# The first unit of weights in quarters on two queues, ones multiplied until the data come, and the first sine layer at another place

## The reference

```
h = rmsnorm(x, norm_mix)
p = h @ w_in                              # 2048 x 4352
h_fwd, h_bwd = implicit_filters(feat, t, w1, b1, fr1, w2, b2, fr2, w3)
#   h = sin(fr1 * (feat @ w1 + b1));  h = sin(fr2 * (h @ w2 + b2));  h = h @ w3;  times a decay
y_a = pool mixer(p[..., :512]);  y_b = hyena mixer(p[..., 512:2816], h_fwd, h_bwd)
y_c = spatial gating(p[..., 2816:])
x = x + concat(y_a, y_b, y_c) @ w_out
x = x + (silu(gate) * val) @ ffn_w_down   # gate, val: width-3 convolutions of rmsnorm(x) @ ffn_w_up
```

## Time and profile before

| | us |
|---|---|
| median of 3 runs | 2247.59 (2247.53 to 2249.07) |
| the profiled execution | 2247.37 |
| its span | 2244.9 |
| TensorE busy in the span | 2206.8 (98%) |

### The profile page before, as it was taken

How to read it: one execution, slowest core, us unless ns; L and a number is a source line. 1 busy time by engine, 2 the same in 40 slices (tenths; PEclk the granted TensorE clock), 3 DMA queues, 4 the chain that set the end, 5 groups by cost and what they waited for, 6 DMA issues and landing times.

```text
span 2244.9 us, 28087 instructions
## 1 busy us (share of the span) xinstructions
PE 2206.8 (98%) x11758; PEld 1883.9 (84%) x11758; DVE 1306.1 (58%) x1593; ACT 1013.3 (45%) x1227; POOL 46.5 (2%) x55
## 2 busy tenths in 40 slices
PE   7999999999999999999999999999999999999998
PEld 6888788888888888888898889878888888888886
DVE  7757547777777775444655555446555555444444
ACT  5443336555555544333654444444433334433333
POOL 1030000000000000000001000000000000000000
PEclk9999999999999999999999999999999999999999
DMA  8444555655555555555464445545666665555552
GB/s 301 158 150 150 182 190 172 204 191 188 189 189 189 190 191 191 192 189 187 142 203 152 151 150 187 183 157 169 188 189 189 189 190 191 193 192 188 188 187 94
DMA packets 267214, 407.55 MB, mean 182 GB/s; under 512 B 6566, under 2 KB 246230, under 8 KB 248657
## 3 DMA queue, kind: packets, MB, share of 16 engines
q1 hardware_dynamic: 264672, 395.47, 53.7%
q0 software_dynamic: 1696, 8.97, 1.1%
q10 hardware_dynamic: 720, 1.32, 0.2%
HBM read 403.64 MB, written 2.10 MB: 181 GB/s over the span
## 4 chain that ended last, share of the span: by engine, by line
PE 94%; DVE 2%; ACT 2%; issue 1%; DMA 1%; DVEq 0%; SPq 0%; ACTq 0%
PE bank L1351 33%; PE bank L1362 17%; PE bank L1386 11%; PE bank L1391 11%; PE bank L1387 11%; PE bank L1354 2%; PE bank L1355 2%; PE bank L1364 2%; DMA raw<-in_w_in 1%; ACT whi L388 1%; DVE wlo L677 1%; PE bank L1241 1%; PE bank L1191 0%; PE bank L1242 0%; ACT M L406 0%
## 5 line engine op out<-in xcount | busy, mean ns | idle before, releaser
L677 DVE TENSOR_TENSOR wlo<-raw,whi 128x2048 fp32r<-128x2048 f32 (+1 forms) x374 | 857.2, 2293 | 815.6 <-ACT whi L388 815.6
L388 ACT ACTIVATE whi<-raw 128x2048 fp32r<-128x2048 f32 (+1 forms) x374 | 715.8, 1916 | 833.2 <-PE bank L1391 446.6
L1351 PE MATMUL bank<-hh,whi 128*128 128x512 f32 x3392 | 825.1, 396 | 14.0 <-ACT whi L388 10.9
L1351 PEld LDWEIGHTS bank<-hh,whi 128*128 128x128 f32 x3392 | 626.5, 189 | 145.9 <-ACT whi L388 10.9
L1362 PEld LDWEIGHTS bank<-hh,wlo 128*128 128x128 f32 x3392 | 429.9, 188 | 17.2
L1362 PE MATMUL bank<-hh,wlo 128*128 128x256 f32 x3392 | 434.8, 281 | 0.0
L1386 PE MATMUL bank<-whi,hh 128*128 128x512 f32 x1088 | 430.6, 396 | 0.0
L1387 PE MATMUL bank<-whi,hh 128*128 128x512 f32 x1088 | 429.0, 394 | 0.0
L1391 PE MATMUL bank<-wlo,hh 128*128 128x512 f32 x1088 | 274.3, 394 | 0.0
L1386 PEld LDWEIGHTS bank<-whi,hh 128*128 128x128 f32 x1088 | 205.5, 189 | 48.6 <-issue 0.2
L1387 PEld LDWEIGHTS bank<-whi,hh 128*128 128x128 f32 x1088 | 205.7, 189 | 46.5
(11 more groups left out here) (221 smaller groups left out, 922.6 us busy)
## 6 DMA issues: line engine op xcount, KB each, us to landing
raw<-in_mlp_w SPq DMA_DIRECT2D x128, 1024.0 KB, 5.4
raw<-in_ffn_w_up SPq DMA_DIRECT2D x88, 1024.0 KB, 5.0
raw<-in_ffn_w_down SPq DMA_DIRECT2D x44, 1024.0 KB, 4.8
raw<-in_w_in SPq DMA_DIRECT2D x34, 1024.0 KB, 5.3
raw<-in_fox_w_in SPq DMA_DIRECT2D x32, 1024.0 KB, 5.3
raw<-in_fox_w_in SPq DMA_DIRECT2D x16, 1032.0 KB, 5.3
raw<-in_w_out SPq DMA_DIRECT2D x16, 1024.0 KB, 4.8
raw<-in_fox_w_out SPq DMA_DIRECT2D x16, 1024.0 KB, 4.8
```

What stands on the lines that cost most here:

```text
L388: e.activation(whi[i % RING][:, 0:n], raw[i % RAW][:, 0:n], ACT.Copy).then_inc(s_hi, 1)
L677: e.tensor_tensor(wlo[i % RING][:, 0:n], raw[i % RAW][:, 0:n], whi[i % RING][:, 0:n].bitcast(F), ALU.subtract).then_inc(s_lo, 1)
L1351: e.matmul(bank[b][:, :], wh[:, k, s], hh[:, kk, :], start=kk == 0, stop=False)
```

## The change

The loads: unit 0 comes as four DMAs of two chunks each on SyncE's queue, X's first half as four DMAs of two chunks each on ScalarE's queue, behind the sixteen columns of the first gain and ahead of the rest of `cols`. ScalarE and VectorE split X and unit 0 quarter by quarter, and TensorE waits for each quarter of unit 0. Unit 1 is split ahead of the second half of X, and the squares come after all of X: four of them, unit 2, the other four. TensorE starts with 32 matmuls of ones. `first_r` goes to place 3 ahead of `filter1`'s matmul. The work of VectorE and ScalarE for the two sine layers is cut from `filter1` and `filter2` and put at places 4 and 6 (`sine1`, `sine2`); TensorE's matmuls stay at 3 and 5. The features and filter weights have a semaphore of their own.

```diff
-    1: [("split", 4), ("spread", 0)], 2: [("total", 0)], 3: [("filter1", 0)], 4: [("first_r", 0)], 5: [("filter2", 0)], 7: [("filter3", 0)],
+    1: [("split", 4), ("spread", 0)], 2: [("total", 0)], 3: [("first_r", 0), ("filter1", 0)], 4: [("sine1", 0)], 5: [("filter2", 0)],
+    6: [("sine2", 0)], 7: [("filter3", 0)],
...
 def sync
-            e.dma_start(X[:, 0:4, :], A["x"][:, 0:4, :]).then_inc(s_x[0], 16)
-            load(0)
-            e.dma_start(X[:, 4:8, :], A["x"][:, 4:8, :]).then_inc(s_x[1], 16)
+            src = units[0][0]
+            for m in range(4):
+                e.dma_start(raw[0][:, 512 * m:512 * m + 512].rearrange("p (k c) -> p k c", k=2), src[:, 2 * m:2 * m + 2, :]).then_inc(
+                    s_w0[m] if m < 3 else s_raw[0], 16)
             load(1)
...
 def scalar
-                    elif what in ("filter1", "filter2"):
-                        o = what == "filter2"
+                    elif what in ("sine1", "sine2"):
+                        o = what == "sine2"
...
-            e.dma_start(cols[:, :], A["cols"]).then_inc(s_col, 16)
+            e.dma_start(cols[:, 0:KD], A["cols"][:, 0:KD]).then_inc(s_gmix, 16)
+            for q in range(4):
+                e.dma_start(X[:, 2 * q:2 * q + 2, :], A["x"][:, 2 * q:2 * q + 2, :]).then_inc(s_x[q], 16)
+            e.dma_start(cols[:, KD:NCOL], A["cols"][:, KD:NCOL]).then_inc(s_col, 16)
             e.wait_ge(s_ones, 1)
             sqrt_table()
+            for q in range(4):
+                s = slice(512 * q, 512 * q + 512)
+                e.wait_ge(s_x[q], 16)
+                high(q, "mix")
+                e.wait_ge(s_w0[q] if q < 3 else s_raw[0], 16)
+                e.activation(whi[0][:, s], raw[0][:, s], ACT.Copy).then_inc(s_hi0 if q < 3 else s_hi, 1)
+            done[0] = 1
+            split(1)
+            for q in range(4, 8):
+                e.wait_ge(s_x[2 + q // 2], 16)
+                high(q, "mix")
             for q in range(8):
                 square(q, piece(q))
+                if q == 3:
+                    split(2)
...
 def vector (low and the subtraction quarter by quarter in the same way), then
+            for q in range(1, 8):
                 add_square(q)
+                if q == 3:
+                    split(2)
...
-                    elif what == "filter1":
-                        e.wait_ge(s_const, 80)
+                    elif what == "sine1":
                         sine(4, col("filt", 0, 64), col("filt", 1, 64))
...
-                    elif what == "filter2":
+                    elif what == "sine2":
                         sine(5, col("filt", 2, 64), col("filt", 3, 64))
...
 def tensor
+            e.wait_ge(s_ones, 1)
+            for _ in range(32):
+                e.matmul(bank[7][:, 0:P], onesr[:, :], onesr[:, :], start=True, stop=True)
```

More of the change, by code:

```diff
@@ L226, in two_block_program @@
         s_hi, s_lo, s_unit = sem("s_hi"), sem("s_lo"), sem("s_unit")
-        s_x = [sem(f"s_x{q}") for q in range(4)]
+        s_x = [sem(f"s_x{q}") for q in range(6)]
+        s_w0 = [sem(f"s_w0{m}") for m in range(3)]
+        s_hi0, s_lo0, s_gmix, s_feat = sem("s_hi0"), sem("s_lo0"), sem("s_gmix"), sem("s_feat")
         s_col, s_id, s_const, s_decay, s_fscale, s_edge, s_ln, s_bs, s_again, s_fox = (
@@ L309, in load @@
                 e.dma_start(dst, src).then_inc(s_raw[i % RAW], 16)
-            e.dma_start(X[:, 0:4, :], A["x"][:, 0:4, :]).then_inc(s_x[0], 16)
-            load(0)
-            e.dma_start(X[:, 4:8, :], A["x"][:, 4:8, :]).then_inc(s_x[1], 16)
+            src = units[0][0]
+            for m in range(4):
+                e.dma_start(raw[0][:, 512 * m:512 * m + 512].rearrange("p (k c) -> p k c", k=2), src[:, 2 * m:2 * m + 2, :]).then_inc(
+                    s_w0[m] if m < 3 else s_raw[0], 16)
             load(1)
-            e.dma_start(X[:, 8:12, :], A["x"][:, 8:12, :]).then_inc(s_x[2], 16)
-            e.dma_start(X[:, 12:16, :], A["x"][:, 12:16, :]).then_inc(s_x[3], 16)
+            e.dma_start(X[:, 8:12, :], A["x"][:, 8:12, :]).then_inc(s_x[4], 16)
+            e.dma_start(X[:, 12:16, :], A["x"][:, 12:16, :]).then_inc(s_x[5], 16)
             for i in range(2, NU):
@@ L331, in gpsimd @@
             e.dma_start(ident[:, :], A["ident"]).then_inc(s_id, 16)
-            for dst, src in ((fe[0:33, :], A["feat"]), (f1, A["filt"]), (w3, A["w3"]), (CS, A["cs"]), (wpool, A["pool_w"])):
+            for dst, src in ((fe[0:33, :], A["feat"]), (f1, A["filt"])):
+                e.dma_start(dst, src).then_inc(s_feat, 16)
+            for dst, src in ((w3, A["w3"]), (CS, A["cs"]), (wpool, A["pool_w"])):
                 e.dma_start(dst, src).then_inc(s_const, 16)
@@ L458, in side @@
                     if what == "spread":
+                        e.wait_ge(s_col, 16)
                         root(1, rb[:, :])
@@ L557, in joined @@
                     square_sum(stage, q, Xt[:, h, 512 * j:512 * j + 512])
-            e.dma_start(cols[:, :], A["cols"]).then_inc(s_col, 16)
+            e.dma_start(cols[:, 0:KD], A["cols"][:, 0:KD]).then_inc(s_gmix, 16)
+            for q in range(4):
+                e.dma_start(X[:, 2 * q:2 * q + 2, :], A["x"][:, 2 * q:2 * q + 2, :]).then_inc(s_x[q], 16)
+            e.dma_start(cols[:, KD:NCOL], A["cols"][:, KD:NCOL]).then_inc(s_col, 16)
             e.wait_ge(s_ones, 1)
             sqrt_table()
-            e.wait_ge(s_col, 16)
-            for q in range(8):
[L564 to L573, removed]
+            e.wait_ge(s_gmix, 16)
+            for q in range(4):
[9 more added lines that the diff above has]
+                high(q, "mix")
+            for q in range(8):
                 square(q, piece(q))
+                if q == 3:
+                    split(2)
             for g, (kind, j, _) in enumerate(IN_GROUPS):
@@ L1040, in joined @@
                 turned(3, gname)
-            e.wait_ge(s_col, 16)
-            for q in range(8):
-                e.wait_ge(s_x[q // 2], 16)
+            e.wait_ge(s_gmix, 16)
+            for q in range(4):
+                s = slice(512 * q, 512 * q + 512)
+                e.wait_ge(s_x[q], 16)
                 low(q, "mix")
[L1046 to L1052, removed]
+                e.wait_ge(*((s_hi0, q + 1) if q < 3 else (s_hi, 1)))
+                e.tensor_tensor(wlo[0][:, s], raw[0][:, s], whi[0][:, s].bitcast(F), ALU.subtract).then_inc(s_lo0 if q < 3 else s_lo, 1)
+            done[0] = 1
+            split(1)
+            for q in range(4, 8):
+                e.wait_ge(s_x[2 + q // 2], 16)
+                low(q, "mix")
+            for q in range(1, 8):
                 add_square(q)
+                if q == 3:
+                    split(2)
             for g, (kind, j, _) in enumerate(IN_GROUPS):
@@ L1259, in side @@
                     elif what == "filter1":
-                        e.wait_ge(s_const, 80)
+                        e.wait_ge(s_feat, 32)
                         e.matmul(bank[4][0:64, 0:T], f1[0:33, 0:64], fe[0:33, :], start=True, stop=True).then_inc(s_fmm, 1)
@@ L1270, in side @@
                         e.wait_ge(s_sin, 2)
+                        e.wait_ge(s_const, 48)
                         e.wait_ge(s_bytok, 1)
@@ L1340, in unit @@
                 wl = wlo[u % RING][:, 0:8 * cw].rearrange("p (k c) -> p k c", k=8)
-                e.wait_ge(s_hi, u + 1)
+                if u:
+                    e.wait_ge(s_hi, u + 1)
                 for k in range(8):
                     kk = half * 8 + k
+                    if u == 0:
+                        e.wait_ge(*((s_hi0, k // 2 + 1) if k < 6 else (s_hi, 1)))
                     if lows is not None:
@@ L1355, in unit @@
                             e.matmul(o, hlo[:, kk, s], wh[:, k, :], start=False, stop=False)
-                e.wait_ge(s_lo, u + 1)
+                if u:
+                    e.wait_ge(s_lo, u + 1)
                 for k in range(8):
                     kk = half * 8 + k
+                    if u == 0:
+                        e.wait_ge(*((s_lo0, k // 2 + 1) if k < 6 else (s_lo, 1)))
                     for n, b in enumerate(pair):
```

## The result

The changed kernel takes 2256.94 us (median of 5 runs, 2255.76 to 2258.38) against 2247.59: a ratio of 1.0040, 95% interval 1.0025 to 1.0054. It is 9.3 us slower, 6 us more than forecast and 3.3 us outside the range. The profiled execution took 2256.84, its span 2254.6.

The account below looks back on a forecast made before the run. TensorE, busy 98% of the span, was taken as the bound, with unit 4's landing chain meeting it at 36 us. 2247.37 + 0 - 1.4 + 3.8 + 1.1 = 2250.9, forecast 2251.0; 8-in-10 range 2246.0 to 2253.6.

Parts of the forecast that it names:

- The quarters, units 1 to 3: Start: unit 0 ends near 13.9 us, 4.6 earlier; the lead shrinks to 1.2 us at unit 3.
- Unit 4's landing: Weight load of unit 4: lands at 29.3 us as before; bounds 2 us earlier to 3.1 us later.
- rival D: GpSimd's transfers or the quarters' descriptors delay unit 4 by 1 to 3.1 us: 2252.2 to 2254.3; chance 0.15.
- The ones at no cost: TensorE's start: 32 matmuls take 3.4 us, end long before the first quarter is down, cost nothing.
- first_r ahead of filter1: TensorE ahead of unit 4: waits for rb until 36.1; unit 4 0.1 us late, unit 5 ends as before.
- The banks' gap: TensorE ahead of unit 6: the 1.40 us wait for group 1's banks goes, a gain of 1.40 us.
- filter2's wait: TensorE behind unit 5: filter2's matmul waits 3.8 us for the Sin, allowed 3.0 to 4.5.
- filter3's wait: TensorE behind unit 7: filter3 waits 1.1 us for the second Sin; unit 8 starts 3.6 us late.
- The sum: Whole profiled execution: start's gain 0, banks' gap -1.4, filter2 +3.8, filter3 +1.1 on 2247.37, giving 2250.9.

Follow-up runs that it names:

- kernels with rb first: Changed kernel, GpSimd's loads behind unit 4, filter matmuls later, VectorE's rb before unit 4's low part: 2245.77 us; without ones 2246.40; with the old start 2248.05.
- order-only kernel: Kernel before with only the new places of first_r and the two sines, nothing of the start: 2252.28 us, ratio 1.0016.

## Why the prediction was wrong

*The quarters, units 1 to 3: right* where it counted. Unit 1 at 15.1 (15.3), unit 2 at 22.2 (22.7), unit 3 at 28.9 (29.0). Unit 0 began at 7.9, not near 6, and ended at 14.9, not 13.9. The ones lasted 7.09 us, 222 ns each, twice the estimate, and held its beginning by some 0.8 us. The copies' and low parts' pace hid that: without the ones unit 0 began at 7.14 and unit 1 at 15.00, against 15.13.

*Unit 4's landing: this step failed.* I took 29.3, with an upper bound of 3.1 us later; it was 4.0 (33.29, past the 31 that the prediction named as a sign of being wrong). I had worked it out as bytes through full engines, and by bytes it is right: unit 3 landed on time. But a landing is complete only when the last of its 16 shares is down, and one share was caught behind GpSimd's burst: 15 by 29.96, the last at 33.27. The rival D named these transfers, but I discounted it since the last square, which releases them, was to end at 24.9 against 24.4 before; it ended at 24.25, and GpSimd issued them at 24.54 against 24.68. D had the cause but not its price: 2252.2 to 2254.3, without the clock. The experiments show that the moment alone doesn't decide: held back, they give 3 us back; with them at 24.38 but no ones there is no loss of that size; the ones alone delay unit 4 by 1 us. The reading that fits all of them is that the 64 additional instructions of TensorE bring an instruction transfer ahead of unit 4's landing, that it makes one engine up to 1 us late, and that the burst does the rest. The shares fit it: in the kernels with rb first, whose burst comes after unit 4, the last share is 0.74 us behind the 15th with the ones, and 0.16 and 0.09 us without an instruction transfer ahead. That it is the same engine no row shows, and in the kernel with no ones, without such a transfer, the last share was still 0.76 us behind; GpSimd's burst began at 28.60 there, ahead of it. So the transfer's part in the 4 us is argued, not shown; shown are GpSimd's 3 us and that without the ones the loss is 0.7 us instead of 4.0.

*The ones at no cost: wrong.* I looked for their cost on TensorE and found cover; it lay in the landing: without them unit 4's copy started 3.3 us earlier.

*first_r ahead of filter1: right* in place (TensorE at rb with both still to do); in the order-only kernel 0.2 us at unit 4 (6.69 us behind unit 3 instead of 6.47) and 0.1 at unit 5.

*The banks' gap and filter2's wait: right.* The gap of 1.40 us went; the wait was 3.46, 3.58 and 3.61 us where rb was near its old place. In the changed kernel it was 1.63, since the slow unit 4 had brought TensorE nearer to the Sin. *filter3's wait:* 1.01 us in the changed kernel (1.1), absent in the three others, whose slow unit 6 took its place.

The sum, corrected for the profiled execution: rb 4.1, clock in unit 4 2.2, the Sin's wait in place of the gap 0.15, filter3's wait 1.0, longer waits up to 250 us 0.4, the stretch from 255 us 1.4. That is 9.3, measured 9.47. Against the 3.5 us forecast, rb and its clock added 6.3 and took 2.2 off filter2's wait.

## What to carry to other kernels

A transfer issued in good time is on the critical path with its slowest share, so ask what else will run on the DMA engines when that share moves: bulk loads of a third queue belong behind the landing that the chain hangs on. An earlier start is worth something only when the next meeting point moves too: here 3.3 us won at unit 1 gave nothing until rb was taken off unit 4's landing. And when work of one engine is moved behind an evacuation, move the matmul that waits for it as well; stalls of 3.5 to 3.6 us cost 5 us in two traces and 6.7 in a third.

## What the runs showed of the hardware that was not expected

- Instructions come by DMA: 16 KB at a time, 1.1 us on one engine; with the 32 matmuls of ones one came at 22.6 to 25.6 us, without them at 29.3 to 32.6.
- While GpSimd's large packets move they hold 77 to 83% of the engines' time, the weights' queue 19 to 25% (stretches 23 to 25 and 29 to 31 us of the kernel before and of the changed one).
- A matmul of 128 columns of ones took 222 ns at the start of the program, and 32 of them did not make unit 0's faster when 2.9 us of idle time lay between (6.00 against 5.94 us).
- The clock fell behind idle stretches of 1.97 and 2.15 us and did not fall behind 2.34 and 2.37 us.
- The lower clock in the stretch from 255 us on lasted 6.6 us in one profiled execution and 10.2 in another, with the same work in it. What decides that stays open.
